# RWKV key norm on 16 rows of head sums, two low-rank matrices side by side on the rows, and unread products on TensorE

## The reference, cut to what matters

```python
r = (xr @ w_r); k = (xk @ w_k); v = (xv @ w_v)
logw = -softplus(-(w0 + tanh(xw @ w1) @ w2)) - 0.5
decay = exp(-exp(logw))
a = sigmoid(a0 + (xa @ a1) @ a2)
kk = (k * k_k).reshape(B, T, 16, 64)
kk = kk / maximum(sqrt(sum(kk * kk, axis=-1, keepdims=True)), 1e-12)
k = k * (1.0 + (a - 1.0) * k_a)
# then, for each token, with the state S of each head:
sa = S @ -kk
S = S * decay + outer(sa, kk * a) + outer(v, k)
y = S @ r
```

## Time and profile before

| what | value |
|---|---|
| median of 3 runs | 2396.66 us (2393.82 to 2401.79) |
| the profiled execution | 2400.18 us |
| its span, first to last instruction | 2398.2 us |
| its mean granted clock of TensorE | 0.907 |
| PE busy | 2116.3 us, 88% of the span |
| DVE busy | 962.8 us, 40% |
| ACT busy | 678.6 us, 28% |
| POOL busy | 154.1 us, 6% |
| the stage at L1621 | 1353.4 to 1424.9 us |

### The profile page before, as it was taken

The page is one execution under the profiler, slowest core; times in us unless marked ns, Lnnn a source line. Parts: engine busy times, 40 slices in busy tenths (PEclk is TensorE's granted clock), DMA queues, the critical chain, the costliest instruction groups (busy, mean ns, idle before and its releaser), DMA issues. The chain is left out here.

```text
span 2398.2 us, 51837 instructions
## 1 busy us (share of the span) xinstructions
PE 2116.3 (88%) x21026; PEld 1889.2 (79%) x21026; DVE 962.8 (40%) x1550; ACT 678.6 (28%) x1152; POOL 154.1 (6%) x240
## 2 busy tenths in 40 slices
PE   4599888878889999996699959999998989999995
PEld 4566556666689999996599739999884689999995
DVE  5323432212244333334943385444514343333334
ACT  2112434344233221221433233323202132212222
POOL 0002201334000000000000000000213100000000
PEclk7797999888999999998899859999977699999997
DMA  3022402455222323321122000001003023232311
GB/s 116 13 62 66 120 1 69 139 150 172 81 71 79 96 67 92 87 75 45 45 82 79 17 0 2 0 0 35 2 6 100 27 62 88 79 115 62 101 56 48
DMA packets 255037, 156.09 MB, mean 65 GB/s; under 512 B 24776, under 2 KB 247855, under 8 KB 254784
## 3 DMA queue, kind: packets, MB, share of 16 engines
q1 hardware_dynamic: 234676, 140.15, 19.9%
q10 hardware_dynamic: 14092, 7.95, 1.1%
q0 software_dynamic: 6144, 6.30, 0.9%
HBM read 148.97 MB, written 5.34 MB: 64 GB/s over the span
## 5 line engine op out<-in xcount | busy, mean ns | idle before, releaser
L311 PE MATMUL ps<-ffn_xh,ffn_wh 128*128 128x280 f32 x1408 | 297.9, 293 | 17.5 <-DVE ffn_xl L1402 13.3
L311 PE MATMUL ps<-ffn_xh,ffn_wl 128*128 128x280 f32 x1408 | 299.3, 294 | 0.0
L311 PE MATMUL ps<-ffn_xl,ffn_wh 128*128 128x280 f32 x1408 | 296.6, 292 | 0.0
L311 PEld LDWEIGHTS ps<-ffn_xh,ffn_wh 128*128 128x128 f32 x1408 | 226.1, 190 | 18.6 <-issue 18.4
L311 PEld LDWEIGHTS ps<-ffn_xh,ffn_wl 128*128 128x128 f32 x1408 | 226.4, 190 | 0.0
L311 PEld LDWEIGHTS ps<-ffn_xl,ffn_wh 128*128 128x128 f32 x1408 | 224.0, 190 | 0.0
L1304 ACT CAST ffn_wh<-wa 128x1024 fp32r<-128x1024 f32 x88 | 91.3, 1041 | 207.9 <-PE ps L311 180.7
L311 PE MATMUL ps<-ffn_hid_h,ffn_wl 128*128 128x280 f32 x704 | 148.3, 292 | 0.0
L311 PE MATMUL ps<-ffn_hid_l,ffn_wh 128*128 128x280 f32 x704 | 147.7, 291 | 0.0
L311 PE MATMUL ps<-ffn_hid_h,ffn_wh 128*128 128x280 f32 x704 | 147.7, 291 | 0.0
L317 DVE TENSOR_TENSOR ffn_wl<-wa,ffn_wh 128x1024 fp32r<-128x1024 f32 x88 | 107.6, 1225 | 86.4 <-ACT ffn_wh L1304 86.4
(11 more groups left out here) (359 smaller groups left out, 3965.5 us busy)
## 6 DMA issues: line engine op xcount, KB each, us to landing
wa<-in_ffn_w_gate SPq DMA_DIRECT2D x44, 512.0 KB, 3.6
wa<-in_ffn_w_up SPq DMA_DIRECT2D x44, 512.0 KB, 3.6
arena<-in_cache_latent SPq DMA_DIRECT2D x104, 128.0 KB, 2.2
wb<-in_ffn_w_down SPq DMA_DIRECT2D x16, 768.0 KB, 4.5
wb<-in_ffn_w_down SPq DMA_DIRECT2D x16, 640.0 KB, 4.3
wb<-in_cache_latent SPq DMA_DIRECT2D x73, 128.0 KB, 2.2
wa<-in_attn_w_o SPq DMA_DIRECT2D x8, 512.0 KB, 4.5
wa<-in_rwkv_w_r SPq DMA_DIRECT2D x8, 512.0 KB, 3.7
```

Source lines behind the costliest of these rows:

```text
L311: mm = nc.tensor.matmul(dst[:, s, 0:HALF], a[:, c * width:(c + 1) * width], b[:, c, s * HALF:(s + 1) * HALF], start=first and n == 0, stop ...
```

## The change

- In `constants`, `spread` becomes 128x1024, the rows from 16 on being zero. The output stage loads its first 16 rows.
- The hidden rows of `a` move from slot 1 of `lora`, partitions 0 to 63, to slot 0, partitions 64 to 127, below which the decay's lie; `a2` is loaded to partitions 64 to 127 of the slot that holds `w2`.
- The norm: ACT squares k times k_k in one pass (`scale=`); PE adds the squares onto 16 rows with `head_window`; DVE takes one maximum and one reciprocal, ACT one square root between the sigmoids of chunk 2 and 3; PE spreads the result with 128-row products against `rs`, which DVE has cleared; DVE multiplies k, k_k and the spread value in one pass out of PSUM. `kk * a` moves to POOL.
- PE's order: two unread products, eight sums, `second` (the low-rank products of one chunk, `a2` and `w2` alternating) for chunks 0 to 3, then spreading and `second` in turn, with an unread product after the spreads of chunks 5, 6 and 7.
- Ten unread products on PE ahead of the scan. An unread product is `ident` times 512 columns of `con`, into banks that are free.

```diff
+        def idle_products(pe, n, bank, cols=512):
+            for _ in range(n):
+                nc.tensor.matmul(ps[:, bank, 0:cols], ident, con[:, 0:cols], start=True, stop=True)
...
+        w2, a2, spread = wa.buf[0][0:64], wa.buf[0][64:P], wa.buf[2]
+        inverse = rs[0:HD]
...
+                sp.dma_start(a2, w["rwkv_a2"][0]).then_inc(l2_in, 16)
                 sp.dma_start(w2, w["rwkv_w2"][0]).then_inc(l2_in, 16)
+                sp.dma_start(spread, w["spread"][0:spread.shape[0]]).then_inc(spread_in, 16)
             def _(pe):
+                idle_products(pe, 2, 2)
+                for m in range(DC):
+                    pe.wait_ge(kk_sq, m + 1)
+                    for s in range(2):
+                        mm = nc.tensor.matmul(ps[0:HD, SUMS_AT + s, 0:HALF], head_window(m), sq[:, m % 2, s * HALF:(s + 1) * HALF],
+                                              start=m == 0, stop=m == DC - 1)
+                    mm.then_inc(kk_summed, 1)
+                def second(m):
+                    ge(pe, a_kept, m)
+                    ge(pe, sw_kept, m)
+                    for s in range(2):
+                        at = slice(s * HALF, (s + 1) * HALF)
+                        ma = nc.tensor.matmul(ps[:, A_AT + s, 0:HALF], a2[:, m * P:(m + 1) * P], lora[64:P, 0, at], start=True, stop=True)
+                        mw = nc.tensor.matmul(ps[:, W_AT + s, 0:HALF], w2[:, m * P:(m + 1) * P], lora[0:64, 0, at], start=True, stop=True)
+                    ma.then_inc(a_done, 1)
+                    mw.then_inc(sw_done, 1)
+                def spread_out(m):
+                    ge(pe, kk_done, m - 1)
+                    for s in range(2):
+                        mm = nc.tensor.matmul(ps[:, SPREAD_AT[m % 2] + s, 0:HALF], spread[:, m * P:(m + 1) * P], rs[:, s],
+                                              start=True, stop=True)
+                    mm.then_inc(kk_spread, 1)
                 pe.wait_ge(l2_in, 32)
+                FIRST = 4
+                for m in range(FIRST):
+                    second(m)
+                pe.wait_ge(spread_in, 16)
+                pe.wait_ge(kk_root, 1)
                 for m in range(DC):
+                    spread_out(m)
+                    if m + FIRST < DC:
+                        second(m + FIRST)
+                    elif m > FIRST:
+                        pe.wait_ge(a_kept, DC)
+                        idle_products(pe, 1, A_AT)
             def _(act):
                 for m in range(DC):
                     ge(act, kk_summed, m - 1)
+                    nc.scalar.activation(sq[:, m % 2], k[:, m], ACT.Square, scale=vcol("k_k", m)).then_inc(kk_sq, 1)
+                for m in range(DC):
+                    act.wait_ge(a_done, m + 1)
+                    nc.scalar.activation(split(av[:, m]), halves(A_AT), ACT.Sigmoid, bias=vcol("a0", m)).then_inc(a_kept, 1)
                     act.wait_ge(sw_done, m + 1)
+                    nc.scalar.activation(split(sg[:, m]), halves(W_AT), ACT.Sigmoid, bias=vcol("w0", m)).then_inc(sw_kept, 1)
+                    if m == 2:
+                        act.wait_ge(kk_mean, 2)
+                        nc.scalar.activation(inverse, inverse, ACT.Sqrt).then_inc(kk_root, 1)
             def _(dve):
+                nc.vector.memset(rs[:], 0.0).then_inc(cleared, 1)
...
+                dve.wait_ge(kk_summed, DC)
+                dve.wait_ge(cleared, 1)
+                nc.vector.tensor_scalar(inverse, ps[0:HD, SUMS_AT:SUMS_AT + 2, 0:HALF], 1e-24, None, ALU.max).then_inc(kk_mean, 1)
+                dve.wait_ge(kk_mean, 1)
+                nc.vector.reciprocal(inverse, inverse).then_inc(kk_mean, 1)
                 dve.wait_ge(less, 1)
                 for m in range(DC):
                     dve.wait_ge(a_kept, m + 1)
                     nc.vector.tensor_scalar(kscale[:, m % 2], av[:, m], vcol("k_a", m), one_less[:, m:m + 1], ALU.mult,
+                                            ALU.add).then_inc(scale_done, 1)
+                    dve.wait_ge(kk_spread, m + 1)
+                    nc.vector.scalar_tensor_tensor(out=split(kk[:, m]), in0=split(k[:, m]), scalar=vcol("k_k", m),
+                                                   in1=halves(SPREAD_AT[m % 2]), op0=ALU.mult, op1=ALU.mult).then_inc(kk_done, 1)
+                    dve.wait_ge(scale_done, m + 1)
                     nc.vector.tensor_tensor(k[:, m], k[:, m], kscale[:, m % 2], ALU.mult).then_inc(k_scaled, 1)
+            def _(pool):
                 for m in range(DC):
+                    pool.wait_ge(kk_done, m + 1)
+                    pool.wait_ge(scale_done, m + 1)
+                    nc.gpsimd.tensor_tensor(av[:, m], kk[:, m], av[:, m], ALU.mult).then_inc(b_done, 1)
...
             def _(pe):
+                idle_products(pe, 10, 1)
                 with pe.Fori(0, NCH) as i:
```

More of the change, by code:

```diff
@@ L120, in constants @@
     put("window", np.arange(4 * DC - 2)[None, :] == 2 * (DC - 1) + p[:, None] // RH, later)
-    spread = np.repeat(np.eye(2 * DC, dtype=np.float32), RH, 1)
+    spread = np.repeat(np.eye(P, 2 * DC, dtype=np.float32), RH, 1)
     return c, later[:, LATER:LATER + NLATER], spread
@@ L1541, in keep @@
                         width, dst = small_cols[n], SMALL[n][4]
-                        nc.scalar.activation(split(lora[0:width, dst]), ps[0:width, 2 * n:2 * n + 2, 0:HALF],
+                        base, dst = (P // 2, 0) if dst == 1 else (0, dst)
+                        nc.scalar.activation(split(lora[base:base + width, dst]), ps[0:width, 2 * n:2 * n + 2, 0:HALF],
                                              [ACT.Tanh, ACT.Copy, ACT.Sigmoid, ACT.Sigmoid][n]).then_inc(cut.kept, 1)
@@ L1612, in program @@
         sg, kk, av = mixed0, mixed1, xx
-        w2, a2 = wa.buf[0][0:64], wa.buf[1][0:64]
+        w2, a2, spread = wa.buf[0][0:64], wa.buf[0][64:P], wa.buf[2]
+        HD = 2 * DC
         sq = wb.buf[0][:, 0:2 * T].rearrange("p (s t) -> p s t", s=2)
         kscale = wb.buf[1][:, 0:2 * T].rearrange("p (s t) -> p s t", s=2)
-        norms = hT
+        inverse = rs[0:HD]
         one_less = wb.buf[1][:, 4 * T:4 * T + DC]
-        l2_in, sw_done, a_done, sw_kept, a_kept = sem("lora2_in"), sem("decay_done"), sem("a_done"), sem("decay_kept"), sem("a_kept")
-        kk_raw, kk_sq, kk_summed, kk_mean, kk_root, kk_done = (sem(f"kk_{n}") for n in ("raw", "squared", "summed", "mean", "root", "done"))
-        k_scaled, b_done, less = sem("k_scaled"), sem("b_done"), sem("one_less")
+        l2_in, spread_in = sem("lora2_in"), sem("spread_in")
+        sw_done, a_done, sw_kept, a_kept = sem("decay_done"), sem("a_done"), sem("decay_kept"), sem("a_kept")
+        kk_sq, kk_summed, kk_mean, kk_root, kk_spread, kk_done = (sem(f"kk_{n}") for n in ("squared", "summed", "mean", "root", "spread", "done"))
+        cleared = sem("rs_cleared")
+        less, scale_done, k_scaled, b_done = sem("one_less"), sem("k_scale"), sem("k_scaled"), sem("b_done")
+        SUMS_AT, A_AT, W_AT, SPREAD_AT = 0, 2, 4, (6, 0)
         with nc.Block(no_gpsimd_drain=True) as block:
@@ L1623, in _ @@
             def _(sp):
+                sp.dma_start(a2, w["rwkv_a2"][0]).then_inc(l2_in, 16)
                 sp.dma_start(w2, w["rwkv_w2"][0]).then_inc(l2_in, 16)
-                sp.dma_start(a2, w["rwkv_a2"][0]).then_inc(l2_in, 16)
+                sp.dma_start(spread, w["spread"][0:spread.shape[0]]).then_inc(spread_in, 16)
             @block.tensor
             def _(pe):
-                pe.wait_ge(l2_in, 32)
-                for m in range(DC):
[L1631 to L1643, removed]
@@ L1683, in program @@
+                pool.wait_ge(b_done, DC)
         bv = av
```

17 lines of the change are left out of this document (2 added, 15 removed).

## The result

The changed kernel takes 2436.03 us (median of four runs, 2433.14 to 2440.88), the kernel before 2399.22 (2393.82 to 2403.72): a ratio of 1.0156, 95% interval 1.0127 to 1.0186, so 37 us slower. I had predicted 2364. In one of the later sessions a single execution of the kernel before took 4579.62 us; it is in no comparison. The profiled execution has a span of 2439.2 us, 41.0 more than before.

The account below looks back on a forecast made before the run. PE at half clock was taken to bound the stage's first 50 us, then DVE the last 17. Stage 29.9 + scan start 4.8 - dip 1.7 = 33.0 us less, giving 2363.7 us; forecast 2359 to 2369 (0.70), range 2359 to 2377 (0.85).

Parts of the forecast that it names:

- What bounds the kernel: Stage between R/K/V products and scan: PE at half clock bounds the first 50 us, then DVE the last 17.
- the steps at full clock: PE product steps at 2.4 GHz: 0.26 us onto 16 rows, 0.475 for 512 columns; eight sums 8.3 us.
- No overlap by rows: Rival, chance 0.12: `a2` and `w2` products on different rows run one after the other in `second`; about 2385 us.
- The dip: PE's clock falls during `second` 0 to 3, where PE waits over half of each beat; 1.7 us, bounds 0 and 5.
- The unread products hold the clock: Two products at the stage's head keep PE's clock up, costing 1.2 us; rival that they do not: 0.08, 2376 us.
- The port: Rival, chance 0.04: POOL's multiply and DVE's two-input multiply in SBUF exclude each other; 2.6 us a chunk, costs 3, 2367.
- DVE's 1.9 us a chunk: End of the stage: scale 0.5, multiply out of PSUM 0.72, k 0.7 on DVE, from 1387.0; kk 7 ready at 1393.5.
- The stage: Whole changed stage: ends at 1395.0 instead of 1424.94, 29.9 us less, if all runs at 2.4 GHz.
- a sign of being wrong: Listed sign against the forecast: POOL's multiplies in the stage taking well over 1.4 us.
- The start of the scan: Ten unread products fit into 9.9 us ahead of the scan; its opening chunk, no longer at low clock, saves 4.8 us.
- The slower rival: Rival, chance 0.03: whole scan stays at low clock, 0.48 lost per low us, gain gone after 69; three low chunks 2412.

Follow-up runs that it names:

- `stage_products_small`: `after_33_small` with the changed stage's five unread products made small, same count of records; 2367.63 us, 0.9861 of the kernel before.
- `after_33_small`: The changed kernel plus 33 small unread products (132 records) at the end of PE's list in the changed stage; 2370.34 us, 0.9875 of the kernel before.

## Why the prediction was wrong

- **What bounds the kernel** was read rightly, and for its own stretch so were the steps at full clock: eight sums in 7.97 us (8.3 put down), a reciprocal of 3.64 on 16 rows (3.65).
- **No overlap by rows** is out: `a2` and `w2` steps start 0.01 us apart.
- **The dip** came where it was put, in the later of the first four `second`s: in the changed kernel's trace the clock is low from about 1371 to 1377. The first multiply out of PSUM starts at 1375.89, where 1374.9 and the 1.7 us of the dip had been put down, so the dip cost about 1.0 up to there.
- **The unread products hold the clock.** The clock stayed up through the sums, but not because of them: in `stage_products_small` it is 1.00 there as well. What the two products bought is a later fall in the `second`s, worth the 1.1 us that they cost. The reason for that rival's 0.08, that sums load only 16 columns, was without weight.
- **The port.** DVE's 1.9 us a chunk was a term of the sum and was mis-sized; to POOL and DVE waiting for each other I gave 0.04 and 3 us. A chunk takes 2.9, since each scale beside POOL's multiply takes 1.61 us, and so DVE was busy without a break from 1376.3 to 1398.2 in `after_33_small`. The stage came out at -25.8 where 29.9 - 1.7 = 28.2 had been put down, 2.4 short: in the changed kernel POOL ends 23.2 us behind the first multiply out of PSUM (1375.89 to 1399.08), not 20.1, and 0.7 of these 3.1 us are made up by the smaller dip. Taking POOL away gave back 1.3 us alone, as PE's low clock was the next bound. The rule of the Trainium skill ("SBUF — State Buffer", Who interferes with whom) that I had quoted against the change agrees with the trace in that one of the two waits for the other. But the pass that pays is the scale, 1.61 against 0.57 us, and not DVE's two-input multiply, which I had named: it takes 0.73 us with POOL and without. POOL's multiply, at 1.80 us, is well over the 1.4 that I had given as a sign of being wrong.
- **The start of the scan** was right within 1.5 us: ten products in 11.3 us, the first 32 steps in 3.68, and 4.4 us gained over the first chunk (24.7 to 29.1), 4.7 in `after_33_small`, where 4.8 had been put down. The products end 1.1 us late, put down as nothing: they began at the low clock (0.77 from 1399.5 to 1410.5), which I had thought unlikely.
- **The step that failed** is one that the sum didn't have. I priced ten products, and the other instructions new on PE, by their run time alone, and took the scan, which the change doesn't touch, as unchanged from its second chunk on. The loop's code had been moved by 119 records, and at each of seven jumps back PE stood still for 4 us while code was fetched and then ran at the low clock for ten or more: 70 us lost against a gain of 29. Without the stalls the same change gains 30 us (`after_33_small`).
- **The slower rival** had the place right, and in part the mechanism: PE in the scan at the low clock, gain used up after 69 low microseconds. The scan has some 85 to 90 of them, which at its 0.48 cost 41 to 43 us; the 28 us of stalls it did not have. And it gave no cause why the clock should fall in the middle of the scan, and "ten full-height products ahead of it" spoke of its start only. Its 0.03 was too little for a case with a part that no row covered.
- **What the profile would have told.** The row of the instruction queue stands on the page of before, and the packets of instructions end after the scan's first round (7 from 1445 to 1472, none from 1475 to 1700), so PE seems to hold the whole loop. 1702 / 256 is 6.65 blocks of 16 KB. "ISA Cache" in "Advanced Engine Details and Errata" of the Trainium skill gives TensorE 128 KB, that is 8 lines of 16 KB or 256 instructions; the packets of 16.4 KB agree. The same section says "Only 2 cache lines!", which does not fit PE here: 6.65 lines run round after round without a packet. And "Instruction fetch mechanics" in "Runtime: NRT & Kernel Launch" says that a taken branch to code outside a window of two pages forces a fetch before execution goes on. The 4.0 us of "issue" at each jump agree with it, and the runs in which no jump stalls show that a loop of this size need not pay. A loop that fills 6.65 of 8 blocks may be one whose place matters, and I should have asked how far the change moves it.

**What stays open.** Where in a block the kernel before begins isn't known, nor how blocks are replaced. A body of 1702 records lies in seven blocks when it starts in the first 91 places of one, and in eight otherwise. Seven blocks and one ahead fit into eight, eight and one ahead do not, and nine packets a jump are as many as that; this agrees with the table, as far as it goes, if before starts just below the edge. It is worked out, not shown, and so is the block of 256 records itself, of which the runs show only that 251, 252 and 256 are harmless and 20 to 123 are not: no run tried an offset between 123 and 251, where the edge on the other side should lie, and why +20 and +40 spoil only some of the jumps is not explained by it.

## What to carry to other kernels

Before inserting instructions ahead of a hardware loop on PE (the other engines were not tried), count the loop's instructions against the code that the engine holds and look at the instruction queue: if its packets stop after the first round, the loop fits, and an insertion can end that. After a change, compare the packets of that queue and the idle time named "issue" at the loop's first instruction; if both have grown, pad by cheap instructions, in a gap, up to a multiple of the block; here 251 to 256 records did it. And price help from POOL with DVE's passes lengthened by it, not only with POOL's own time.

## What the runs showed of the hardware

- A jump back that has to fetch costs 3.7 to 4.3 us of standing still in the changed kernel and 3.0 to 4.0 with 123 increments in the kernel before, and 5 to 6 us more through the clock: 32 steps of L1836 take 6.42 to 7.06 us behind it instead of 3.79. The low clock is the larger part.
- Five tiny products, 20 records, cost some 33 us (two runs); 64 of them cost nothing.
- A semaphore increment on PE takes about 0.15 us: 123 of them hold the scan's first product until 19.1 us after the block opened (1445.88 - 1426.79). A small product of 8 columns is four records and takes 1.81 / 33 = 0.055 us, so as padding it is some eleven times cheaper per record.
- DVE's scale of 560 columns takes 1.61 us beside a multiply on POOL and 0.57 in the same place without it; POOL's multiply 1.80 beside it and 1.37 in rows 8.
- Products on rows 0 to 63 and 64 to 127 start 0.01 us apart even when two whole products of the first kind are written ahead of the second.
- Products onto 16 rows, 128 deep, hold the clock at 1.00 by themselves over the 8 us that they take (1353.4 to 1363.0 in `stage_products_small`).
